# Softmax weights divided by their sum before they are turned, and values in two matmul passes for three

## The reference, cut to what matters

```
p = softmax(where(allowed, q @ k.T, -inf), axis=-1)    # per head, 512 queries x 512 keys
o = p @ v                                              # v: 512 x 64
```

## Time and profile before

| | |
|---|---|
| median of three runs | 1711.18 us |
| profiled execution, its own time | 1711.5 us |
| span of its records | 1709.7 us |
| PE (matmul) busy | 1688.6 us, 99% |
| DVE (VectorE) busy | 1272.5 us, 74% |
| ACT (ScalarE) busy | 957.2 us, 56% |
| mean granted TensorE clock | 0.997 of full |

### The profile page before, as it was taken

How to read it: one execution, slowest core, us unless ns; L and a number is a source line. 1 busy time by engine, 2 the same in 40 slices (tenths; PEclk the granted TensorE clock), 3 DMA queues, 4 the chain that set the end, 5 groups by cost and what they waited for, 6 DMA issues and landing times.

```text
span 1709.7 us, 25289 instructions
## 1 busy us (share of the span) xinstructions
PE 1688.6 (99%) x9375; PEld 1459.4 (85%) x9375; DVE 1272.5 (74%) x2020; ACT 957.2 (56%) x1645; POOL 169.8 (10%) x147
## 2 busy tenths in 40 slices
PE   9999999999999999999999999999999999999998
PEld 7888877888788897789899988878887999999977
DVE  6378877776567776589698986775566978898966
ACT  4267875665436666478556364652235866464655
POOL 2011212000300000220000002320003000000041
PEclk9999999999999999999999999999999999999999
DMA  8222124214243222243232433313322432323621
GB/s 270 84 73 74 40 73 101 75 50 148 75 110 76 74 75 81 74 173 117 81 121 81 145 152 132 99 62 103 114 91 87 161 123 99 99 99 100 234 75 50
DMA packets 152786, 177.52 MB, mean 104 GB/s; under 512 B 18281, under 2 KB 126342, under 8 KB 150886
## 3 DMA queue, kind: packets, MB, share of 16 engines
q1 hardware_dynamic: 150790, 159.22, 29.8%
q10 hardware_dynamic: 1888, 16.85, 2.5%
HBM read 158.82 MB, written 12.58 MB: 100 GB/s over the span
## 4 chain that ended last, share of the span: by engine, by line
PE 88%; DVE 8%; ACT 3%; issue 1%; DMA 1%; DVEq 0%; SPq 0%; ACTq 0%
PE bank L1158 27%; PE bank L1159 26%; PE bank L1160 26%; PE bank L1507 2%; DVE split_weights L2671 2%; PE bank L1531 1%; PE bank L1426 1%; DVE act_b L2671 1%; PE bank L1415 1%; DMA raw_weights<-in_w_mlp_down 1%; DVE act_a L2673 0%; PE bank L1823 0%; ACT act_a L1920 0%; DVE work L2706 0%; PE bank L1341 0%
## 5 line engine op out<-in xcount | busy, mean ns | idle before, releaser
L1158 PE MATMUL bank<-act_a,split_weights 128*128 128x512 f32 (+1 forms) x1360 | 525.4, 386 | 6.3 <-DVE act_a L2671 2.0
L1160 PE MATMUL bank<-act_a,split_weights 128*128 128x512 f32 (+1 forms) x1360 | 518.8, 381 | 0.0
L1159 PE MATMUL bank<-act_a,split_weights 128*128 128x512 f32 (+1 forms) x1360 | 518.1, 381 | 0.0
L1158 PEld LDWEIGHTS bank<-act_a,split_weights 128*128 128x128 f32 x1360 | 256.0, 188 | 58.5 <-issue 6.1
L1160 PEld LDWEIGHTS bank<-act_a,split_weights 128*128 128x128 f32 x1360 | 255.6, 188 | 50.3
L1159 PEld LDWEIGHTS bank<-act_a,split_weights 128*128 128x128 f32 x1360 | 256.0, 188 | 45.1 <-issue 0.2
L1158 PE MATMUL bank<-act_b,split_weights 128*128 128x256 f32 (+1 forms) x648 | 207.4, 320 | 0.3 <-DVE split_weights L3355 0.2
L1160 PE MATMUL bank<-act_b,split_weights 128*128 128x256 f32 (+1 forms) x648 | 206.4, 318 | 0.0
L1159 PE MATMUL bank<-act_b,split_weights 128*128 128x256 f32 (+1 forms) x648 | 206.3, 318 | 0.0
L2613 DVE TENSOR_TENSOR split_weights<-raw_weights,split_weights 128x2048 fp32r<-128x2048 f32 x55 | 127.1, 2311 | 76.1 <-ACT split_weights L1865 63.3
L1865 ACT ACTIVATE split_weights<-raw_weights 128x2048 fp32r<-128x2048 f32 x51 | 97.3, 1908 | 119.5 <-PE bank L1160 119.5
(11 more groups left out here) (356 smaller groups left out, 3261.5 us busy)
## 6 DMA issues: line engine op xcount, KB each, us to landing
raw_weights<-in_w_mlp_up SPq DMA_DIRECT2D x32, 1024.0 KB, 5.4
...
```

Of the source, the lines that this page charges most:

```text
L1158: nc.tensor.matmul(dst, w[0], a[0], start=first, stop=False)
L1159: nc.tensor.matmul(dst, w[0], a[1], start=False, stop=False)
L1160: mm = nc.tensor.matmul(dst, w[1], a[0], start=False, stop=last)
```

## The change

In both softmax attentions:

1. The exponential also writes the sum of its row (`accum_out`) into `row_sums`.
2. A new VectorE step n follows (`inverse`): the reciprocal of the 128 row sums, a wait for it, and a multiplication of the step's row in `tmp` by it, in place. `turn` waits for n (`normed`), not for e.
3. The stationary columns that held ones now hold the low part of V (`values_lo` writes them), so one 128-column pass by the high weights gives high V in rows 0 to 63 and low V in rows 64 to 127. A second pass of 64 columns multiplies high V by the low weights. The third pass goes. The same form is used by the stick-breaking attention already.
4. ScalarE's Ln and Exp after the values become one copy of rows 64 to 127 (`parts_out`), and VectorE's multiplication in `gather` becomes an addition. The memsets of ones and zeros go.
5. VectorE's order strings get n0 to n7. TensorE's and ScalarE's strings are as before.

```diff
-        DVE_MLA = "m0 m1 m2 m3 p0 p1 p2 m4 p3 m5 c0 c1 c2 y1 m6 p4 c3 m7 p5 s2 p6 g0 p7 y2 x0 x1 s3 g1"
+        DVE_MLA = "m0 m1 n0 m2 n1 m3 p0 n2 p1 n3 p2 m4 p3 m5 c0 n4 c1 n5 c2 y1 m6 p4 n6 c3 m7 p5 s2 n7 p6 g0 p7 y2 x0 x1 s3 g1"
-        DVE_FOX = "m0 m1 c0 m2 c1 p0 m3 s2 p1 m4 m5 p2 p3 y0 m6 c2 m7 c3 y1 p4 p5 g0 p6 p7 x0 x1 s3 g1"
+        DVE_FOX = "m0 m1 c0 n0 m2 n1 c1 p0 m3 n2 s2 p1 m4 n3 m5 p2 p3 y0 n4 m6 n5 c2 m7 n6 c3 y1 p4 p5 n7 g0 p6 p7 x0 x1 s3 g1"
-        DVE_NEAR = "m0 m1 m2 m3 p0 y0 c0 c1 p1 p2 m4 m5 p3 m6 c2 c3 o0 o1 p4 y1 m7 p5 g0 x0 x1 p6 p7 s2"
+        DVE_NEAR = "m0 n0 m1 n1 m2 m3 p0 y0 c0 n2 c1 p1 n3 p2 m4 m5 p3 n4 m6 n5 c2 n6 c3 o0 o1 p4 y1 m7 p5 n7 g0 x0 x1 p6 p7 s2"
-        DVE_LAST = "m0 m1 m2 h1 p0 m3 s1 o2 y0 p1 o3 c0 p2 m4 o4 y1 p3 o5 m5 c1 m6 m7 c2 c3 p4 p5 o6 g0 p6 p7 g1"
+        DVE_LAST = "m0 m1 n0 m2 h1 p0 n1 m3 s1 n2 o2 y0 n3 p1 o3 c0 p2 m4 o4 y1 p3 n4 o5 m5 n5 c1 m6 n6 m7 c2 n7 c3 p4 p5 o6 g0 p6 p7 g1"
...
                 def turn(i, s):
-                    pe.wait_ge(A["exp"], 8 * i + s + 1)
+                    pe.wait_ge(A["normed"], 8 * i + s + 1)
...
-                        three(banks[5][:, c:S], [head_v[:, hh, hl, kt, :] for hl in (0, 1)],
-                              [act_b[:, hl, kt, c:S] for hl in (0, 1)], kt == 0, kt == TT - 1,
-                              A["out"] if kt == TT - 1 else None)
+                        out_, v = banks[5][:, c:S], head_v[:, hh, 0, kt, :]
+                        if kt:
+                            nc.tensor.matmul(out_[0:HD, :], v[:, 0:HD], act_b[:, 1, kt, c:S], start=False, stop=False)
+                        mm = nc.tensor.matmul(out_, v, act_b[:, 0, kt, c:S], start=kt == 0, stop=kt == TT - 1)
+                        if kt == 0:
+                            nc.tensor.matmul(out_[0:HD, :], v[:, 0:HD], act_b[:, 1, kt, c:S], start=False, stop=False)
+                    mm.then_inc(A["out"], 1)
...
                     nc.scalar.activation(tmp[:, s % 4, 0:(j + 1) * P], score_bank(s)[:, 0:(j + 1) * P], ACT.Exp,
-                                         bias=negmax[:, s:s + 1]).then_inc(A["exp"], 1)
+                                         bias=negmax[:, s:s + 1], accum_out=row_sums[:, s:s + 1]).then_inc(A["exp"], 1)
-                def invert_sums(i, hh):
-                    h = 2 * i + hh
-                    act.wait_ge(A["out"], FREE + h + 1)
-                    nc.scalar.activation(sum_inverse(hh), banks[5][HD:2 * HD, :], ACT.Ln).then_inc(A["sum_log"], 1)
-                    act.wait_ge(A["sum_log"], h + 1)
-                    nc.scalar.activation(sum_inverse(hh), sum_inverse(hh), ACT.Exp, scale=-1.0).then_inc(A["sum_inverse"], 1)
+                def parts_out(i, hh):
+                    act.wait_ge(A["out"], FREE + 2 * i + hh + 1)
+                    nc.scalar.activation(low_rows(hh), banks[5][HD:2 * HD, :], ACT.Copy).then_inc(A["parts_copied"], 1)
...
-                    dve.wait_ge(A["sum_inverse"], 2 * i + hh + 1)
-                    V.tensor_tensor(dst, src, sum_inverse(hh), ALU.mult).then_inc(A["gathered"], 1)
+                    dve.wait_ge(A["parts_copied"], 2 * i + hh + 1)
+                    V.tensor_tensor(dst, src, low_rows(hh), ALU.add).then_inc(A["gathered"], 1)
...
+                def inverse(i, s):
+                    dve.wait_ge(A["exp"], 8 * i + s + 1)
+                    V.reciprocal(row_sums[:, s:s + 1], row_sums[:, s:s + 1]).then_inc(A["sum_inverse"], 1)
+                    dve.wait_ge(A["sum_inverse"], 8 * i + s + 1)
+                    part = tmp[:, s % 4, 0:(s % TT + 1) * P]
+                    V.tensor_scalar(part, part, row_sums[:, s:s + 1], None, ALU.mult).then_inc(A["normed"], 1)
...
-            for hl, value in ((0, 1.0), (1, 0.0)):
-                V.memset(head_v[:, :, hl, :, HD:2 * HD].bitcast(F32), value)
```

More of the change, by code:

```diff
@@ L287, in hybrid_block_kernel @@
         negmax = sb("negmax", [P, 8])
+        row_sums = sb("row_sums", [P, 8])
         banks = [ctx.enter_context(nc.psum_tensor(f"bank{i}", [P, S], F32)) for i in range(8)]
@@ L406, in hybrid_block_kernel @@
         STICK_ONLY = ("clipped", "softplus", "masked", "rows_added", "part_hi", "part_ready", "summed", "w_exp")
-        SOFTMAX_ONLY = ("turned", "negmax", "pt_hi", "pt_ready", "w_begun", "v_hi", "v_staged", "sum_log", "sum_inverse",
+        SOFTMAX_ONLY = ("turned", "negmax", "pt_hi", "pt_ready", "w_begun", "v_hi", "v_staged", "sum_inverse", "parts_copied",
                         "gated")
@@ L457, in hybrid_block_kernel @@
         ACT_MLA = "e0 e1 y1 p0 e2 p1 w0 e3 p2 p3 s2 w1 e4 e5 p4 y2 e6 p5 e7 p6 r0 p7 s3 r1"
[L458 removed]
+        DVE_MLA = "m0 m1 n0 m2 n1 m3 p0 n2 p1 n3 p2 m4 p3 m5 c0 n4 c1 n5 c2 y1 m6 p4 n6 c3 m7 p5 s2 n7 p6 g0 p7 y2 x0 x1 s3 g1"
         PE_FOX = "z0 g0 z1 g1 z2 t0 t1 z3 g2 z4 t2 g3 z5 t3 g4 z6 t4 t5 z7 v0 g5 t6 t7 g6 g7 v1"
         ACT_FOX = "w0 y0 e0 e1 w1 p0 e2 s2 p1 e3 p2 p3 e4 e5 y1 e6 s3 p4 p5 e7 r0 p6 p7 r1"
[L461 removed]
+        DVE_FOX = "m0 m1 c0 n0 m2 n1 c1 p0 m3 n2 s2 p1 m4 n3 m5 p2 p3 y0 n4 m6 n5 c2 m7 n6 c3 y1 p4 p5 n7 g0 p6 p7 x0 x1 s3 g1"
         PE_NEAR = "z0 z1 z2 g0 g1 t0 t1 z3 g2 z4 t2 z5 g3 t3 z6 g4 t4 t5 v0 g5 z7 g6 g7 t6 t7 a0 v1"
         ACT_NEAR = "y0 e0 e1 p0 p1 e2 w0 w1 e3 p2 p3 e4 e5 e6 o0 o1 p4 p5 y1 r0 e7 p6 p7 s2 r1"
[L466 removed]
+        DVE_NEAR = "m0 n0 m1 n1 m2 m3 p0 y0 c0 n2 c1 p1 n3 p2 m4 m5 p3 n4 m6 n5 c2 n6 c3 o0 o1 p4 y1 m7 p5 n7 g0 x0 x1 p6 p7 s2"
         PE_LAST = "z0 z1 z2 g1 t0 z3 t1 g2 t2 t3 z4 z5 z6 g3 t4 z7 g4 v0 t5 g5 t6 t7 g6 v1"
         ACT_LAST = "e0 s1 p0 e1 y0 e2 o2 e3 p1 o3 w0 p2 y1 o4 p3 e4 o5 w1 e5 o6 e6 e7 p4 p5 r0 p6 p7 r1"
[L471 removed]
+        DVE_LAST = "m0 m1 n0 m2 h1 p0 n1 m3 s1 n2 o2 y0 n3 p1 o3 c0 p2 m4 o4 y1 p3 n4 o5 m5 n5 c1 m6 n6 m7 c2 n7 c3 p4 p5 o6 g0 p6 p7 g1"
         ACT_MLA_LAST = "e0 e1 y1 p0 e2 p1 w0 e3 p2 p3 w1 e4 e5 p4 o0 e6 p5 o1 e7 p6 r0 p7 o2 r1"
[L474 removed]
+        DVE_MLA_LAST = "m0 m1 n0 m2 n1 m3 p0 n2 p1 n3 p2 m4 p3 m5 c0 n4 c1 n5 c2 y1 m6 p4 n6 c3 m7 p5 o0 n7 p6 g0 o1 p7 x0 x1 o2 g1"
         EARLY_OUT = {"mla": 3, "fox": 7}
@@ L534, in halves, with low_rows @@
             return slice(hh * HD, (hh + 1) * HD), slice((1 - hh) * HD, (2 - hh) * HD)
-        def sum_inverse(hh):
+        def low_rows(hh):
             return sq[hh * HD:(hh + 1) * HD, 0, :]
@@ L2213, in pair_of_heads @@
                         elif what == "r":
-                            invert_sums(pair, s)
+                            parts_out(pair, s)
                         elif what == "e":
@@ L2852, in values_lo @@
                 dve.wait_ge(hi_done, count)
-                lo = head_v[:, hh, 0, :, HD:2 * HD] if kind == "sb" else head_v[:, hh, 1, :, 0:HD]
-                low(lo, head_values(kind, i, hh), head_v[:, hh, 0, :, 0:HD], lo_done)
+                low(head_v[:, hh, 0, :, HD:2 * HD], head_values(kind, i, hh), head_v[:, hh, 0, :, 0:HD], lo_done)
             def rest_halves(part, value, which):
@@ L3090, in pair_of_heads @@
                             maxima(pair, s)
+                        elif what == "n":
+                            inverse(pair, s)
                         elif what == "c":
```

1 line of the change is left out of this document (removed).

## The result

The changed kernel takes 1744.6 us (median of 4 runs, 1744.34 to 1745.36) against 1711.1 us for the kernel before (4 runs, 1710.29 to 1711.73): ratio 1.0197, 95% interval 1.0179 to 1.0214, slower by 33.5 us. The forecast was 1739.6 us, in a range of 1722 to 1756.

A forecast was written before the change was run, and what follows sets the result against it. The prediction took TensorE alone to bound the attention stages. New waits of 44 us less 15.5 saved (+12.3 + 13.4 + 0.8 + 1.9 = +28.4) on 1711.2 gave 1739.6 us, range 1722 to 1756.

The forecast's parts named there:

- TensorE's saving: Values of each head: two passes take 1.28 us instead of 1.93, saving 0.65 a head, 15.5 us for 24 heads.
- n's price: New VectorE step: reciprocal 0.15 us, multiplication 0.28 to 0.48 by width; 0.46 to 0.66 us from start to result.
- the rival with the rate of a bank: In-place multiplication in n runs at the bank's 0.745 us for 512 columns: 1752 us in all, chance 0.08.
- The sum of each row: ScalarE's accum_out: 0.1 us taken per exponential, between bounds of nothing and 0.20.
- The walk through a fox pair: Steady fox pairs: new waits at turnings of 3.35 us less 1.3 saved, +2.05 us a pair, six times, 12.3.
- The walk through an MLA pair: MLA pairs: new waits at turnings of 4.65 us less 1.3 saved, +3.35 us a pair, four times, 13.4.
- The waits in the profile: Profile after: PE idle before turnings, released by VectorE's multiplication, 35 to 45 us in all.
- the last two pairs: Seventh and eighth fox pairs: waits of 2.05 and 3.2 us, less 1.3 saved in each, +0.8 and +1.9.
- Only the steps behind their own z wait: Rival: no VectorE queue builds up, waits mainly at fox t1, t5 and MLA t1; 1714.6 us, chance 0.12.
- Faster: Rival: VectorE is early enough at fox t1 and t5, only 7.2 us of waits; 1702.9 us, chance 0.05.
- The clock falls too: Rival: new pauses in MLA pairs, perhaps fox pairs, lower PE's clock, adding 6.4 to 16 us; 1746 to 1756, chance 0.13.

The follow-up runs named there:

- e1: Changed kernel without the division (no row sums, no n, no wait for n), two-pass values kept: 1694.97 us, ratio 0.9909.
- e8: Changed kernel without the exponentials' sums; row_sums set to 1.0 once, n still runs: 1742.76 us.
- e3: Changed kernel with n writing its product to an unread tile and the turning waiting for the exponential alone: 1721.28 us, ratio 1.0059.
- e6: Changed kernel with new step orders on TensorE, ScalarE and VectorE for MLA pairs and all fox pairs, including the last two: 1704.86 us, ratio 0.9963.
- e2: Kernel before, three passes and ones columns kept, plus row sums, n and the turning's wait for n: 1755.36 us, ratio 1.0259.
- e9: Kernel before (three passes, no division) with the new step orders of e6: 8.0 us slower than with the old orders.
- e12: Kernel before plus the division and its wait, three passes kept, in the orders of e6: 6.4 us above the 1720.5 expected.
- e10: Changed kernel without the division, two-pass values kept, in the orders of e6: 5.4 us slower than e1 with the old orders.

## Why the prediction was right, point by point

**Right: the sign, the mechanism and the size.** 28.4 us were forecast, 33.5 measured. In the sum two errors cancel, which is luck: the MLA stage came out 1.2 us under its term and the first six fox pairs 1.1 over.

**TensorE's saving.** 0.65 us a head forecast, 0.68 measured by e1 (16.4 for 24 heads, in which the shorter r and a clock that stays at 1.00 in the last pair are contained). The steady pairs show it without the clock: 1.3 us an MLA pair and 1.4 a fox pair. The values of a head take the 1.28 us of the forecast.

**n's price.** Reciprocal 0.15 forecast, 0.157 measured. Multiplication 0.28, 0.35, 0.42 and 0.48 forecast, 0.288, 0.354, 0.421 and 0.486 measured; the rival with the rate of a bank is out. The tile is overwritten in place and still keeps the rate of the rows. By the Trainium skill (VectorE: DVE Perf Modes, section Mode 2×_2P) an operation with a single source, fp32 too, takes two elements a cycle where source and destination are in SBUF. The 0.486 us with source and destination the same, against 0.484 with two tiles, agree.

**The sum of each row.** 0.1 us forecast on the exponential's end, as a middle of two bounds. It is an operation of 0.196 behind it, which begins 0.1 before the exponential has ended (574.23 against 573.96 + 0.37 in the rows above). The delay of 0.1 was right; e8 shows that it counts for 1.8 us in all.

**The walk through a fox pair.** In the forecast t1, t3, t4 with t5, and t7 are 1.2, 0.15, 1.35 and 0.6 late. Measured, with 0.2 to each bracket: 1.16, 0.37, 1.32 and 0.59. The sum is 3.44, and the difference of the pairs of after and e1 is 3.6. The forecast's own four terms add up to 3.30, not to the 3.35 that it wrote; over six pairs that is 0.3 us. The forecast put the whole second loss on t5; part of it sits on t4, because n4 really is late behind p2, p3 and y0, as its text had it.

**The walk through an MLA pair.** t1, t3, t4, t6, t7: forecast 0.55, 0.65, 0.5, 1.4, 1.55; measured, in the same way, 0.49, 0.57, 0.55, 1.39, 1.58. The sum is 4.58 against 4.65.

**The waits in the profile.** 35 to 45 us of idle time ahead of turnings were forecast, and the view shows 30.5. With 0.2 us for each of its 50 pauses it is 40.5.

**Mis-sized: the last two pairs.** Their term was 0.8 + 1.9 = 2.7 us. The offset between the two timelines gives what it really was. It is 12.2 us behind the MLA stage. At v0 of the sixth fox pair it is 26.3, where t7 of that pair (0.6) is still to come and the shorter values of both heads are still to be saved (1.3), so 25.6 at its end. PE's first wait behind the attention, before and after, shows 31.8:

```profile
726.66 0.47 PE L1158 MATMUL bank<-act_a,split_weights 128*128 128x512 f32 x1 [0.17 <-ACT work L2282]
```

```profile
758.50 0.47 PE L1159 MATMUL bank<-act_a,split_weights 128*128 128x512 f32 x1 [0.20 <-ACT work L2284]
```

So the last two pairs took 6.2 us, 3.5 more than their term. The first six took 25.6 - 12.2 = 13.4 for 12.3, and the MLA stage 12.2 for 13.4.

Against e1, whose clock stays at 1.00 in the last pair, the last two pairs (with the same correction for t7) lose 10.4 us: 49.9 at the wait behind the attention less 38.9 at v0 of the sixth pair and 0.6. The forecast had 2.05 + 3.2 = 5.25 for these waits. It counted the delays of n in the last pair, and it left out that the clock falls twice there, beside pauses grown from 2.04 to 2.73 us and joined by one of 2.36; that took some 3 us. The other 2 are longer waiting.

**Left out: 1.3 us behind the attention.** The offset over the whole span is 33.1, 1.3 more than at that wait. PE's later waits are a little longer at the same places, 0.54 us for 0.36 at 825 us and 0.79 for 0.21 at 1071 us, the second for low parts of weights. At this second place e1, e3 and e6 wait 1.1 to 1.3 us, and e2, e9 and e12, with three passes, have no wait of 0.15 or more. Why two-pass kernels wait there is not shown.

**The rivals.** "Only the steps behind their own z wait" is refuted: t3, t6, t7 wait too, and t6 and t7 of MLA are the longest pauses of the steady pairs. "Faster" is refuted at its own place, t1. "The clock falls too" did not happen where I priced it: the pauses of 1.19 and 1.38 us in MLA pairs and of 0.96 in fox pairs left it at 1.00. It did happen in the last pair, where I had given the clock no term beyond what the kernel before already lost.

**Where the expected gain went.** The 16.4 us saved on PE are real (e1), with 1.7 of clock in them. The division is nearly free as work: 4.5 us once the orders leave it room, although VectorE carries the same instructions. What it cost with the old orders, 49.6, was the order: half the new wait, half the queue behind n (e3), and 45.1 of it went away with a change of order alone (e6 less e10 is 4.5). The new orders cost 5.4 us of their own (e10 less e1), so 39.7 of the 45.1 are left in the time. About 3 us of these savings are the clock in the last pair, which fell in the changed kernel and not in e6, e1 or e10.

What stays open: the last fox pair. e6 leaves 7.2 us of pauses there, and my one try at it made it worse. Also open are what makes the clock fall in one execution of that pair and not in another, and the 1.3 us behind the attention.
